# Moving the conditioning products of a two-layer decoder between the weight pieces, in column-grouped units

## The chip, the cores and the metric

One core of a Trainium2 chip runs the whole program. The metric is the device time of one execution in microseconds. Three runs of the kernel before gave a median of 3252.13 us (3251.81 to 3252.35).

## The reference, cut to what matters

Two decoder layers run over 544 tokens: one prompt of 512 and eight sequences of four sample tokens. Each layer is a half-step SwiGLU feed-forward block (FFN1), a middle block (input projection, an RG-LRU recurrence, sparse attention with a top-k index, output projection) and a second half-step block (FFN2). Before each block the residual is normalised, scaled and shifted, and after each block a normalised result is added with a gate. The nine scale, shift and gate vectors of a layer come from one product with the conditioning vectors `c` (9 rows: the prompt and eight sequences):

```python
mod = (c @ w_ada_l + b_ada_l).reshape(c.shape[0], N_MOD, -1)
sh1, sc1, gt1, sh2, sc2, gt2, sh3, sc3, gt3 = [mod[:, m][:, None, :] for m in range(N_MOD)]
f = swiglu(rms_norm(x, g[0]) * (1 + sc1) + sh1, w_gu[0], w_dn[0])
x = x + 0.5 * gt1 * rms_norm(f, g[1])
h = rms_norm(x, g[2]) * (1 + sc2) + sh2
...
x = x + gt2 * rms_norm(y, g[3])
f = swiglu(rms_norm(x, g[4]) * (1 + sc3) + sh3, w_gu[1], w_dn[1])
x = x + 0.5 * gt3 * rms_norm(f, g[5])
```

All of it is float32; `D_MODEL` is 1024, `D_FF` 2816, `w_ada` is 1024 x 9216 in each layer.

## The kernel before, in words

Everything is kept transposed: features on the 128 partitions, the 544 tokens in the free dimension, in two halves of 272. All five engines run streams written by hand, tied by semaphores; the two layers are unrolled.

**Weight pieces.** A weight matrix is used in pieces of 128 columns. A piece is loaded by the SP queue (`piece`, L470 to L477) into one of four raw slots `wslot`. ScalarE rounds it to a high part `w_hi` (L874, `split`), VectorE subtracts to get a low part (L1110, `split`), and TensorE multiplies high by high, high by low and low by high (L581, L582, L583, in `piece`), for each of the two token halves and each of eight row chunks: 48 products of 272 columns. There are two high and two low buffers. SP loads a raw slot again when VectorE has made the low part from it (`w_split`, L476). A feed-forward block has 44 gate-up pieces (GU) and 24 down pieces (DN), the down pieces with 8, 8 and 6 row chunks for each of eight output columns. The input projection (IN) has 17 pieces and the output projection (OUT) eight.

**Ada.** `w_ada` goes through the same four raw slots, 72 pieces a layer. `ada_chunk` (L586 to L594) multiplies one piece with `c`: the stationary operand is `cT` (128 x 9), the moving one 128 columns of `w_ada`, eight products over the rows, plain float32. For each of the nine vectors VectorE copies the two halves of the result (L1198, `ada_half`), TensorE transposes them (L601), and VectorE adds the bias (L1204, `ada_bias`). The order is written out by hand: vectors 0 and 1 at the start of a layer (`ADA0`), 2 to 4 between GU and DN of FFN1 (`ADA1`, L624 `between()`), and 5 to 8 in the sample top-k loop of the attention (`ADA2`, L794 to L801, one chunk in each of the 32 iterations).

**Around the blocks.** After the last down piece TensorE sums the squares of the eight result chunks with a matrix of ones (`sums_of_squares`, L547 to L555, products at L553, plain float32), ScalarE takes the root (L858), VectorE the reciprocal and the residual (`residual`, L1138 to L1157), then the squares of the new `x` are summed the same way, and `pre_norm` (L1113 to L1136) writes the next block's moving operands chunk by chunk.

**The top-k loop.** VectorE runs 32 iterations of MAX8 (L1495) and MATCH_REPLACE8 (L1508) over the sample scores, with the prompt attention's masked maximum (L1488), `tile_output` (L1471), `ada_half` and `ada_bias` between them. After it come L1510, the last `tile_output`, the mask transposes (L807) and L1517.

**Queues.** SP issues nearly all loads in program order: `cT`, `x`, the constants and the page table, then the pieces, 16 small gate loads (L513), half of the key pages, and the value pages of three sequences (L531) with `ADA2` pieces between them. The POOL queue loads the other key and value pages.

Of the kernel before, what the change touches and what calls it, by code (L numbers as in the profile page):

```python
# [18 lines left out]
F32 = mybir.dt.float32  # L19
# [52 lines left out]
RING = 4  # L72
RPF = DC // RING
U_GU = FC // 2
DN_K = (8, 8, 6)


class Phase:


    full = [0] * RING
    ada = [0] * RING
    split = [0] * RING
    used = [0, 0]
    order = 0

    def __init__(self, rounds, per_round, slots, is_ada=False, tail=0):
        self.rounds, self.per_round, self.slots, self.tail = rounds, per_round, slots, tail
        self.full0, self.ada0, self.split0 = list(Phase.full), list(Phase.ada), list(Phase.split)
        self.used0, self.order0 = list(Phase.used), Phase.order  # L90
        for n in range(rounds * per_round + tail):
            i = n % slots
            Phase.full[i] += 1
            (Phase.ada if is_ada else Phase.split)[i] += 1
            if not is_ada:
                Phase.used[n % 2] += 1
                Phase.order += 1

    def has(self, u, n):

        return u * self.per_round + n < self.rounds * self.per_round + self.tail

    def raw(self, u, n):

        return n % self.slots, u * (self.per_round // self.slots) + n // self.slots

    def part(self, u, n):

        return n % 2, u * (self.per_round // 2) + n // 2


ADA0 = Phase(2 * RPF, RING, RING, is_ada=True)
GU1 = Phase(U_GU, RING, RING)
ADA1 = Phase(3 * RPF, RING, RING, is_ada=True)
DN1 = Phase(DC // 2, 2 * len(DN_K), len(DN_K))
IN = Phase(PC // RING, RING, RING, tail=1)
ADA2 = Phase(4 * RPF, RING, RING, is_ada=True)
OUT = Phase(DC // RING, RING, RING)
GU2 = Phase(U_GU, RING, RING)
DN2 = Phase(DC // 2, 2 * len(DN_K), len(DN_K))  # L120
PAGE_UNROLL = 4
ARENA = FC * T + 2048
KREC = PAGE + PAGE // 2


DVE_STEPS = 361
# [14 lines left out]
def hold(eng, passed, sem, value):  # L141


    eng.wait_ge(sem, value)
    eng.sem_inc(passed, 1)


class Steps:

    def __init__(self, eng, sem, per, layer, passed):
        self.passed = passed
        self.eng, self.sem, self.per, self.layer, self.n, self.shift = eng, sem, per, layer, 0, 0
# [7 lines left out]
    def need(self, n):  # L162

        self.eng.wait_ge(self.sem, self.layer * self.per + (n + self.shift))

    def need_hold(self, n):

        hold(self.eng, self.passed, self.sem, self.layer * self.per + (n + self.shift))
# [3 lines left out]

    def link_hold(self, ins):

        self.need_hold(self.mark(ins))

    @contextmanager
    def loop(self, times, body_steps, start=0):

        first = self.n  # L180
        with self.eng.Fori(start, start + times) as i:
            self.shift = i * body_steps + (-start * body_steps)
            yield i
        assert self.n - first == body_steps, (self.n - first, body_steps)
        self.n = first + times * body_steps
        self.shift = 0


def decoder(nc, a):

    with ExitStack() as ctx:
# [10 lines left out]
        wslot = [sb(f"wslot{i}", [P, DC, P]) for i in range(RING)]  # L202
# [17 lines left out]
        act_hi = part("act_hi", at_arena, FC, T)  # L220
        at_whi = at_arena + FC * T
        w_hi = [part(f"w_hi{i}", at_whi + i * DC * P, DC, P) for i in range(2)]
        h_hi = part("h_hi", at_proj, DC, T)
        h_lo = part("h_lo", at_h, DC, T)
        at_wlo = at_proj + DC * T
        w_lo_ffn = [part(f"w_lo_ffn{i}", at_wlo + i * DC * P, DC, P) for i in range(2)]
        at_tsil = at_wlo + 2 * DC * P
        at_alo = at_down + 2 * PAGES * KREC - FC * T
        assert at_tsil + 2 * T <= at_alo and at_whi + 2 * DC * P <= at_proj
        act_lo = part("act_lo", at_alo, FC, T)  # L230

# [3 lines left out]
        w_lo_mid = [part(f"w_lo_mid{i}", at_whi - (2 - i) * DC * P, DC, P) for i in range(2)]  # L235
        cst = sb("cst", [P, C_ALL])
        vec = sb("vec", [P, V_ALL])
        state = sb("state", [P, ST_ALL])
        cT = sb("cT", [P, DC, NC_])
        mod = sb("mod", [P, MC, NC_])  # L240
        modT = sb("modT", [NC_, DC, P])
# [7 lines left out]

        sq = proj[:, 0:DC, :]  # L250
        tsil = part("tsil", at_tsil, 2, T, dt=F32)
# [23 lines left out]
        assert at_arena + at[0] <= at_whi - 2 * DC * P  # L275
# [48 lines left out]
        w_full = [sig(f"w_full{i}", Phase.full[i], 16) for i in range(RING)]  # L324
        ada_used = [sig(f"ada_used{i}", Phase.ada[i]) for i in range(RING)]
        w_hi_done = sig("w_hi_done", Phase.order)
        w_split = [sig(f"w_split{i}", Phase.split[i]) for i in range(RING)]
        w_used = [sig(f"w_used{i}", Phase.used[i]) for i in range(2)]
        vec_full = sig("vec_full", 2, 16)
        vec_free = sig("vec_free", 1, 1, 1)  # L330
        gate_full = sig("gate_full", 16, 16)
# [10 lines left out]
        modT_ready = sig("modT_ready", 2 * NMOD)  # L342
        mod_pe = sig("mod_pe", NMOD)
        ada_read = sig("ada_read", NMOD, 1, 1)
# [6 lines left out]
        act_raw = sig("act_raw", 2 * FC)  # L351
# [4 lines left out]
        act_ready = sig("act_ready", 2 * FC, 1, 2)  # L356
# [54 lines left out]
        cleared = sig("cleared", 0)  # L411
        passed = [ctx.enter_context(nc.semaphore(f"passed_{e}")) for e in ("sp", "pe", "pool", "dve")]
# [29 lines left out]
        def key_loads(eng, on_sp, l, pair):  # L442


            who, first, after, full = ((passed[0], 0, KEYS_SP, kp_full) if on_sp
                                       else (passed[2], KEYS_SP, PAGES, kp_full_pool))
            if isinstance(pair, int):

                hold(eng, who, dn_read.sem, dn_read.at(l, DC))
            for i in range(2):  # L450
                hold(eng, who, kp_used[i].sem, kp_used[i].at(l, pair))
                load_pages(eng, a["key_pages"], l, pair * (2 * PAGES) + i * PAGES, first, after, kpage[i], full[i])
# [3 lines left out]
        def _(sp):  # L456
            sp.dma_start(cT[:, :, :], a["cT"]).then_inc(s_in.sem, 16)
            sp.dma_start(x[:, :, :], a["xT"]).then_inc(s_in.sem, 16)
            sp.dma_start(cst[:, :], a["cst"]).then_inc(s_in.sem, 16)
            sp.dma_start(pages[:, :], a["page_table"]).then_inc(s_in.sem, 16)  # L460
            sp.wait_ge(s_in.sem, 64)
            sp.wait_ge(cleared.sem, 1)
            for l in range(DEPTH):

                def rows(ap):
                    return ap.rearrange("a (c p) n -> p (a c) n", p=P)

                ada, w_in, w_out = (layer_of(a[n], l) for n in ("w_ada", "w_in", "w_out"))

                def piece(ph, u, n, src):  # L470

# [7 lines left out]
                def pieces(ph, src, first=0, start=0, rounds=None):  # L479

                    for u in range(start, start + (rounds or ph.rounds)):
                        for n in range(RING):
                            piece(ph, u, n, rows(src[:, :, bass.ds(u * (RING * P) + (first + n) * P, P)]))
# [1180 lines left out]
```

## Time and profile before

| | |
|---|---|
| median of three runs | 3252.13 us |
| the profiled execution | 3247.81 us |
| its span, first to last instruction | 3246.1 us |
| TensorE busy | 88% of the span, 20506 products |
| VectorE / ScalarE / GpSimd busy | 45% / 23% / 5% |
| granted TensorE clock, mean | 0.89 of full speed |
| DMA | 292.75 MB, 90 GB/s, 524771 packets |

A busy share says how much of the span had an instruction of that engine in flight; the ends of products are modelled. The profiled execution is 4.3 us (0.13%) shorter than the median. The execution falls into these stages in layer 0 (layer 1 repeats them from about 1627 us): start to 73.6, GU of FFN1 to 344.6, `ADA1` to 393.8, DN to 528, residual and norm to 570, IN to 687, recurrence and index products to 873, top-k loop to 1055, the rest of the attention to 1118, OUT to 1170, residual and norm to 1211, GU and DN of FFN2 to 1619.

### The profile page before, as it was taken

To read this page: it belongs to the slowest core of one execution; us is meant where nothing else is said; L and a number is where in the kernel's file an instruction comes from. 1 tells how busy PE (TensorE), PEld (TensorE's weight loads), DVE (VectorE), ACT (ScalarE), POOL (GpSimd) and SP (SyncE) were. 2 spreads that over 40 slices of the span, in tenths; PEclk is the share of its full clock that TensorE was granted. 3 is DMA by queue.
4 is the path that set the end of the run, shared out by engine and by line. 5 is a ranking of instruction groups with operands and counts; after the bars stand their busy time and mean duration, and the time that the engine had idled before them with its cause. 6 is when DMAs were issued, how large, how long until landed. Compare 5 with 4: busy or idle time off the path is not lost.

```text
span 3246.1 us, 49665 instructions
## 1 busy us (share of the span) xinstructions
PE 2854.9 (88%) x20506; PEld 2638.2 (81%) x20506; DVE 1465.4 (45%) x2006; ACT 734.3 (23%) x1038; POOL 158.8 (5%) x298
## 2 busy tenths in 40 slices
PE   5999997988778669999979999969796868699997
PEld 4999896976655669999969998969675548699997
DVE  2333124365799443332153331244648992533312
ACT  1222023230012132222222220222200222322221
POOL 0000001001420000000000000010114100000000
PEclk8999998975579789999999999989656889899998
DMA  6232623212353012222243326323124421132231
GB/s 186 83 88 86 183 87 85 73 40 64 115 152 111 20 46 84 86 87 76 87 130 88 89 85 184 90 68 83 48 67 127 141 83 46 39 91 86 71 90 64
DMA packets 524771, 292.75 MB, mean 90 GB/s; under 512 B 20673, under 2 KB 518882, under 8 KB 524162
## 3 DMA queue, kind: packets, MB, share of 16 engines
q1 hardware_dynamic: 513154, 266.35, 28.1%
q0 software_dynamic: 11392, 23.23, 2.4%
q8 instruction: 161, 2.64, 0.3%
q14 instruction: 64, 0.52, 0.1%
HBM read 285.75 MB, written 3.77 MB: 89 GB/s over the span
## 4 chain that ended last, share of the span: by engine, by line
PE 81%; DVE 14%; issue 3%; DMA 1%; ACT 1%; SPq 0%; DVEq 0%; ACTq 0%
PE ps L583 20%; PE ps L581 20%; PE ps L582 19%; PE ps L592 5%; PE ps L703 4%; PE ps L553 3%; DVE sb_arena L1495 3%; PE ps L701 3%; DVE sb_y L1508 3%; PE ps L819 2%; PE ps L563 1%; DMA sb_wslot<-w_ada 1%; DVE sb_h L1122 1%; PE ps L723 1%; DVE sb_h L1149 1%
## 5 line engine op out<-in xcount | busy, mean ns | idle before, releaser
L582 PE MATMUL ps<-sb_h_lo,sb_w_hi 128*128 128x272 f32 x3360 | 972.8, 290 | 0.0
L581 PE MATMUL ps<-sb_h_hi,sb_w_hi 128*128 128x272 f32 x2816 | 817.7, 290 | 54.6 <-DVE sb_h_lo L1135 54.6
L583 PE MATMUL ps<-sb_h_hi,sb_w_lo_ffn 128*128 128x272 f32 x2816 | 820.1, 291 | 0.0
L1110 DVE TENSOR_TENSOR sb_w_lo_ffn<-sb_wslot,sb_w_hi 128x1024 fp32r<-128x1024 f32 (+1 forms) x272 | 324.0, 1194 | 792.3 <-ACT sb_w_hi L874 792.1
L874 ACT ACTIVATE sb_w_hi<-sb_wslot 128x1024 fp32r<-128x1024 f32 (+2 forms) x322 | 332.8, 1036 | 1518.4 <-PE ps L583 1380.0
L582 PEld LDWEIGHTS ps<-sb_h_lo,sb_w_hi 128*128 128x128 f32 x3360 | 640.5, 191 | 0.5
L581 PEld LDWEIGHTS ps<-sb_h_hi,sb_w_hi 128*128 128x128 f32 x2816 | 534.3, 190 | 59.6 <-issue 53.8
L583 PEld LDWEIGHTS ps<-sb_h_hi,sb_w_lo_ffn 128*128 128x128 f32 x2816 | 533.8, 190 | 0.0
L581 PE MATMUL ps<-sb_act_hi,sb_w_hi 128*128 128x272 f32 x1408 | 408.5, 290 | 11.1 <-DVE sb_w_lo_ffn L1110 11.1
L583 PE MATMUL ps<-sb_act_hi,sb_w_lo_ffn 128*128 128x272 f32 x1408 | 407.9, 290 | 0.0
L582 PE MATMUL ps<-sb_act_lo,sb_w_hi 128*128 128x272 f32 x1408 | 407.4, 289 | 0.0
L592 PE MATMUL ps<-sb_wslot,sb_cT 128*9 128x128 f32 x2304 | 301.0, 294 | 20.6 <-DMA sb_wslot<-w_ada 20.5
L592 PEld LDWEIGHTS ps<-sb_wslot,sb_cT 128*9 128x9 f32 x2304 | 217.8, 98 | 87.0 <-issue 19.5
L581 PEld LDWEIGHTS ps<-sb_act_hi,sb_w_hi 128*128 128x128 f32 x1408 | 268.4, 191 | 11.6 <-issue 11.6
L582 PEld LDWEIGHTS ps<-sb_act_lo,sb_w_hi 128*128 128x128 f32 x1408 | 268.5, 191 | 0.0
L583 PEld LDWEIGHTS ps<-sb_act_hi,sb_w_lo_ffn 128*128 128x128 f32 x1408 | 268.4, 191 | 0.0
L1173 DVE SCALAR_TENSOR_TENSOR sb_tsil<-sb_tsil,ps 128x544 f32<-128x544 f32 x88 | 63.4, 721 | 276.3 <-PE ps L583 276.3
L581 PE MATMUL ps<-sb_h_hi_mid,sb_w_hi 128*128 128x272 f32 x544 | 162.3, 298 | 27.0 <-DVE sb_h_lo L1135 27.0
L433 POOL DMA_DIRECT2D sb_down<-key_pages x128 | 68.8, 538 | 1970.8 <-issue 1970.8
L703 PE MATMUL ps<-sb_arena,sb_down 128*128 128x32 f32 x512 | 161.6, 409 | 0.0
L583 PE MATMUL ps<-sb_h_hi_mid,sb_w_lo_mid 128*128 128x272 f32 x544 | 158.4, 291 | 0.0
L1495 DVE MAX8 sb_arena<-sb_y 32x8 f32<-32x2080 f32 x64 | 147.9, 2311 | 0.0
(217 smaller groups left out, 3152.0 us busy)
## 6 DMA issues: line engine op xcount, KB each, us to landing
sb_wslot<-ffn_w_gu SPq DMA_DIRECT2D x176, 512.0 KB, 3.6
sb_wslot<-w_ada SPq DMA_DIRECT2D x144, 512.0 KB, 4.8
sb_wslot<-ffn_w_down SPq DMA_DIRECT2D x64, 512.0 KB, 3.9
sb_wslot<-w_in SPq DMA_DIRECT2D x32, 512.0 KB, 3.8
sb_wslot<-ffn_w_down SPq DMA_DIRECT2D x32, 384.0 KB, 3.3
sb_down<-key_pages POOLq DMA_DIRECT2D x128, 96.0 KB, 2.2
sb_down<-key_pages SPq DMA_DIRECT2D x128, 96.0 KB, 1.9
sb_wslot<-w_out SPq DMA_DIRECT2D x16, 512.0 KB, 4.1
```

The source lines that it names most:

```text
L433: eng.dma_start(dst.rearrange("p a n -> p (a n)"), src).then_inc(full.sem, 16)
L553: last = mm(ps[:, 6 + b, 0:TH], ones, sq[:, c, b * TH:(b + 1) * TH], start=(c == 0), stop=(c == DC - 1))
L581: mm(out, wh, xh, start=(kc == 0), stop=False)
L582: mm(out, wh, xl, start=False, stop=False)
L583: last = mm(out, wl, xh, start=False, stop=(kc == of - 1))
L592: last = mm(ps[0:NC_, bank, i * P:(i + 1) * P], cT[:, kc, :], wslot[i][:, kc, :], start=(kc == 0), stop=(kc == DC - 1))
L701: mm(ps[0:HD, 4 + i, j * 32:(j + 1) * 32], kpage[i][:, j, P:KREC], qiS[:, bass.ds(pair * 2 + i, 1), :, :].rearrange("p a e c -> p (a e c)" ...
L703: last = mm(ps[:, 6 + i, j * 32:(j + 1) * 32], kpage[i][:, j, 0:P], qS[:, bass.ds(pair * 2 + i, 1), :].rearrange("p a c -> p (a c)"), star ...
L874: act_fn(w_hi[s][:, 0:rows, 0:cols], wslot[i][:, 0:rows, 0:cols], ACT.Copy).then_inc(w_hi_done.sem, 1)
L1110: v.tensor_tensor(w_lo[s][:, 0:rows, 0:cols], wslot[i][:, 0:rows, 0:cols], w_hi[s][:, 0:rows, 0:cols].bitcast(F32), ALU.subtract).then_inc ...
L1495: found = st.mark(v.max(top_s, scS))
L1508: replaced = st.mark(v.match_replace(scS, top_s, scS, TAKEN))
```

## The change

- Ada becomes 18 units of 512 columns a layer. A unit is 32 products: for each of eight row chunks, four products whose outputs lie on partitions 0 to 31, 32 to 63, 64 to 95 and 96 to 127. `cT` is padded to 32 columns. One VectorE copy of 128 x 128, one 128 x 128 transpose and one bias addition finish a unit.
- Units 0 to 3 run at the start of layer 0, each with its own buffer. Units 4 to 15 of each layer run in GU of FFN1, one behind every third piece. Units 16 and 17, and in layer 0 also the first four of layer 1, run in GU of FFN2, one behind every sixth piece. They share one 2 MB buffer `ada_w`; SP loads it again when the products of the unit before are done. A unit is transposed one piece later.
- `ADA1` and `ADA2` are gone from the gap behind GU and from the top-k loop.
- The low part of a piece overwrites its raw slot. There are three high buffers, and SP loads piece q when product q - 4 is done (`w_used`). Splits run two pieces ahead across the ends of blocks.
- Gate-up products use three pairs of PSUM banks and wait for the reads of the piece three before. DN waits for the activations that its first pieces need, not for all.
- In DN and OUT the squares of a result column are summed behind a piece of the next column; the last column's behind the last piece.
- Weights and `w_ada` are laid out by the host so that a piece or unit is one contiguous row for each partition; `vec` and `state` of both layers and the gates come in one load each. `hold` (a wait followed by a semaphore increment) becomes a plain wait.

```diff
+            def unit(n, pair):
+                buf = ada_first[n] if n < 4 else ada_w
...
                 for kc in range(DC):
-                    last = mm(ps[0:NC_, bank, i * P:(i + 1) * P], cT[:, kc, :], wslot[i][:, kc, :],
-                              start=(kc == 0), stop=(kc == DC - 1))
-                last.then_inc(ada_used[i].sem, 1)
+                    for g in range(4):
+                        last = mm(ps[32 * g:32 * (g + 1), 2 * pair, 0:P], cT[:, kc, :], buf[:, kc, g * P:(g + 1) * P],
+                                  start=(kc == 0), stop=(kc == DC - 1))
+                last.then_inc(ada_mm.sem, 1)
+            def unit_transpose(n, pair):
+                pe.wait_ge(ada_tok.sem, n + 1)
+                if n:
+                    pe.wait_ge(ada_done.sem, n)
+                nc.tensor.transpose(ps[:, 2 * pair + 1, 0:P], modT[:, :], ident).then_inc(ada_pe.sem, 1)
...
+            def ffn(l, f):
...
+                for n in range(GU_N):
+                    if n >= 3:
+                        pe.wait_ge(gu_read.sem, reads + n - 2)
+                    piece(q + n, 1 + n % 3, h_hi, h_lo, norm=2 * f if n == 0 else None)
+                    if n - 1 in units:
+                        unit_transpose(units[n - 1], 0)
+                    if n in units:
+                        unit(units[n], 0)
...
+                for n in range(DN_N):
+                    m, j = divmod(n, len(DN_K))
+                    k0 = sum(DN_K[:j])
+                    if m == 0:
+                        pe.wait_ge(act_ready.sem, act_ready.at(l, f * FC + k0 + DN_K[j]))
...
+                    piece(q + n, dn_pair(m), act_hi, act_lo, k0, FC)
+                    if m and j == 1:
+                        squares_of(m - 1, dn_read, l, f * DC)
+                squares_of(DC - 1, dn_read, l, f * DC).then_inc(ss_ready.sem, 1)
...
+                for n in range(OUT_N):
+                    pe.wait_ge(wo_read.sem, wo_read.at(l, n + 1 - 2))
+                    piece(l * PIECES + OUT + n, n % 2, y_hi, y_lo)
+                    if n:
+                        squares_of(n - 1, wo_read, l, 0)
+                squares_of(OUT_N - 1, wo_read, l, 0).then_inc(ss_ready.sem, 1)
-                sums_of_squares(wo_read, l, 0)
...
+            def unit(n):
+                if n > 4:
+                    sp.wait_ge(ada_mm.sem, n)
+                dst = ada_first[n] if n < 4 else ada_w
+                sp.dma_start(dst.rearrange("p c n -> p (c n)"), a["w_ada"][n // UNITS, n % UNITS])\
+                    .then_inc((ada_full0[n] if n < 4 else ada_full).sem, 16)
+            sp.dma_start(cT[:, :, :], a["cT"]).then_inc(c_in.sem, 16)
+            unit(0)
...
+            sp.dma_start(cst[:, :], a["cst"]).then_inc(s_in.sem, 16)
+            unit(1)
+            sp.dma_start(x[:, :, :], a["xT"]).then_inc(x_in.sem, 16)
+            unit(2)
+            unit(3)
...
+                def piece(q, src):
+                    rows, cols = shape_of(q)
+                    if q >= SLOTS:
+                        sp.wait_ge(w_used.sem, q - SLOTS + 1)
...
+                        if n - 1 in units:
+                            unit_bias(units[n - 1], 0)
+                        if n in units:
+                            unit_token(units[n], 0)
...
-                    if hd == 4:
-                        ada_half(5 + i, 0, ADA2, i * RPF + 1, 0)
-                    if i and hd == 0:
-                        ada_half(5 + i - 1, 1, ADA2, i * RPF, 0)
-                    if i and hd == 2:
-                        ada_bias(5 + i - 1, 1)
```

## Rows read from the trace of the kernel before

**Rows 1.** The page's part 4: the chain that ended last, by engine.

```profile
PE 81%; DVE 14%; issue 3%; DMA 1%; ACT 1%; SPq 0%; DVEq 0%; ACTq 0%
```

**Rows 2.** Busy times by stretch: length, PE, PEld, DVE, ACT, POOL, clock, DMA, GB/s.

```profile
78.00:344.00 266.00, 266.00 (x2096) 265.79 (x2095) 94.98 (x108) 68.78 (x86) 0.00 (x0) 0.99 0.29 84
344.00:392.00 48.00, 45.42 (x414) 36.60 (x412) 5.99 (x10) 1.75 (x3) 0.00 (x0) 1.00 0.86 249
```

**Rows 3.** Timeline of GU: start us, us, instruction; the last products of neighbouring pieces.

```profile
199.83 0.28 PE L583 MATMUL ps<-sb_h_hi,sb_w_lo_ffn 128*128 128x272 f32 x1
...
205.87 0.28 PE L583 MATMUL ps<-sb_h_hi,sb_w_lo_ffn 128*128 128x272 f32 x1
```

**Rows 4.** Timeline, layer 0: first product of `ADA1` and first of DN.

```profile
344.62 14.14 PE L592 MATMUL ps<-sb_wslot,sb_cT 128*9 128x128 f32 x128
...
393.84 0.47 PE L581 MATMUL ps<-sb_act_hi,sb_w_hi 128*128 128x272 f32 x1 [1.67 <-DVE sb_w_lo_ffn L1110]
```

**Rows 5.** Chain in order of time (start us, us), layer 1: the same two places.

```profile
1949.86 3.61 PE ps L592 x32
...
1997.89 0.36 PE ps L581
```

**Rows 6.** Chain: last product of GU, first two of DN, FFN2 of layer 0.

```profile
1480.24 0.14 PE ps L583
...
1484.23 0.57 PE ps L581
1484.80 0.23 PE ps L582
```

**Rows 7.** Timeline: sums of squares behind DN and the next block's first product, twice.

```profile
1619.41 7.49 PE L553 MATMUL ps<-sb_proj,sb_cst 128*128 128x272 f32 x32
...
1680.64 0.57 PE L581 MATMUL ps<-sb_h_hi,sb_w_hi 128*128 128x272 f32 x1 [13.06 <-DVE sb_h_lo L1135]
...
528.13 7.50 PE L553 MATMUL ps<-sb_proj,sb_cst 128*128 128x272 f32 x32
...
528.85 0.62 ACT L916 ACTIVATE sb_proj<-ps 128x544 f32<-128x544 f32 x1
...
569.63 0.56 PE L581 MATMUL ps<-sb_h_hi_mid,sb_w_hi 128*128 128x272 f32 x1 [13.06 <-DVE sb_h_lo L1135]
```

**Rows 8.** Timeline of VectorE: the top-k loop's first two iterations, and its end.

```profile
876.62 0.29 DVE L1488 CUSTOM_DVE_ANT_0 sb_arena<-ps,sb_arena 128x128 f32<-128x128 f32 x1 [1.05 <-PE ps L746]
...
881.60 0.27 DVE L1488 CUSTOM_DVE_ANT_0 sb_arena<-ps,sb_arena 128x128 f32<-128x128 f32 x1
...
1048.51 1.23 DVE L1510 TENSOR_SCALAR sb_y<-sb_y 32x2080 f32<-32x2080 f32 x1
...
1054.84 0.69 DVE L1517 COPY sb_rinv<-ps 128x512 f32<-128x512 f32 x1 [0.81 <-PE ps L808]
```

**Rows 9.** Timeline of the start: first use of `x`, sums of squares, first product.

```profile
12.46 4.48 ACT L853 ACTIVATE sb_proj<-sb_x 128x544 f32<-128x544 f32 x8 [9.54 <-DMA sb_pages<-page_table]
...
52.92 7.57 PE L553 MATMUL ps<-sb_proj,sb_cst 128*128 128x272 f32 x32 [0.42 <-DVE sb_mod L1204]
...
73.55 0.57 PE L581 MATMUL ps<-sb_h_hi,sb_w_hi 128*128 128x272 f32 x1 [13.06 <-DVE sb_h_lo L1135]
```

**Rows 10.** DMA issues by line: count, KB each, us from issue to landing.

```profile
sb_x<-xT SPq DMA_DIRECT2D x1, 2176.0 KB
sb_cst<-cst SPq DMA_DIRECT2D x1, 1072.0 KB
sb_wslot<-ffn_w_gu SPq DMA_DIRECT2D x176, 512.0 KB, 3.6
sb_vec<-vec SPq DMA_DIRECT2D x2, 76.0 KB, 1.8
```

**Rows 11.** Ada products: their group by line, and one chunk of 16 in `ADA1`.

```profile
L592 PE MATMUL ps<-sb_wslot,sb_cT 128*9 128x128 f32 x2304 | 301.0, 294 | 20.6 <-DMA sb_wslot<-w_ada 20.5
...
372.65 1.92 PE L592 MATMUL ps<-sb_wslot,sb_cT 128*9 128x128 f32 x16 [0.16 <-DMA sb_wslot<-w_ada]
```

More of the change, by code:

```diff
@@ L68, with dn_pair, shape_of @@
 ST_H, ST_C, ST_ALL = 0, LC * NSEQ, LC * NSEQ * 4
-RING = 4
-RPF = DC // RING
-U_GU = FC // 2
+SLOTS, HIS = 4, 3
+GU_N, DN_N, OUT_N = 2 * FC, 3 * DC, DC
 DN_K = (8, 8, 6)
[L78 to L120, printed above, removed]
+GU1 = 0
+DN1 = GU1 + GU_N
+IN = DN1 + DN_N
+OUT = IN + PC + 1
+GU2 = OUT + OUT_N
+DN2 = GU2 + GU_N
+PIECES = DN2 + DN_N
+UNITS = 18
+UNIT = 512
+UNITS_IN = [[(l * UNITS + 4 + i, 3 * i + 2) for i in range(12)] for l in range(DEPTH)], \
+           [[(l * UNITS + 16 + i, 6 * i + 5) for i in range(6) if l * UNITS + 16 + i < DEPTH * UNITS] for l in range(DEPTH)]
+def dn_pair(m):
+    return 1 + (m - 1) % 2 if m else 3
+def shape_of(q):
+    n = q % PIECES
+    if DN1 <= n < IN or n >= DN2:
+        return DN_K[(n - (DN1 if n < IN else DN2)) % len(DN_K)], P
+    return DC, LAST if n == OUT - 1 else P
 PAGE_UNROLL = 4
-ARENA = FC * T + 2048
+ARENA = 13928 + 88
 KREC = PAGE + PAGE // 2
-DVE_STEPS = 361
 class Signal:
@@ L162, in need @@
     def need(self, n):
-        self.eng.wait_ge(self.sem, self.layer * self.per + (n + self.shift))
-    def need_hold(self, n):
-        hold(self.eng, self.passed, self.sem, self.layer * self.per + (n + self.shift))
+        self.eng.wait_ge(self.sem, n)
     def link(self, ins):
         self.need(self.mark(ins))
[L173 to L186, printed above, removed]
 def decoder(nc, a):
@@ L323, in decoder @@
         s_in = sig("s_in", 0)
[L324 to L331, printed above, removed]
+        c_in = sig("c_in", 0)
+        x_in = sig("x_in", 0)
+        w_full = [sig(f"w_full{i}", 0) for i in range(SLOTS)]
+        w_hi_done = sig("w_hi_done", PIECES)
+        w_split = sig("w_split", PIECES)
+        w_used = sig("w_used", PIECES)
+        ada_full0 = [sig(f"ada_full0{i}", 0) for i in range(4)]
+        ada_full = sig("ada_full", 0)
+        ada_mm = sig("ada_mm", UNITS)
+        ada_tok = sig("ada_tok", UNITS)
+        ada_pe = sig("ada_pe", UNITS)
+        ada_done = sig("ada_done", UNITS)
+        gu_read = sig("gu_read", 2 * GU_N)
+        gate_full = sig("gate_full", 1, 16)
         KEYS_SP = 8
@@ L463, in _ @@
+            sp.dma_start(x[:, :, :], a["xT"]).then_inc(x_in.sem, 16)
+            unit(2)
+            unit(3)
             for l in range(DEPTH):
[L465 to L470, printed above, removed]
-                    i, k = ph.raw(u, n)
-                    is_ada = ph in (ADA0, ADA1, ADA2)
-                    before = (ph.ada0[i], k + ph.split0[i]) if not is_ada else (k + ph.ada0[i], ph.split0[i])
-                    hold(sp, passed[0], ada_used[i].sem, ada_used[i].at(l, before[0]))
-                    sp.wait_ge(w_split[i].sem, w_split[i].at(l, before[1]))
-                    sp.dma_start(wslot[i][:, 0:src.shape[1], 0:src.shape[2]], src).then_inc(w_full[i].sem, 16)
```

577 lines of the change are left out of this document (254 added, 323 removed).

## The prediction, made before the changed kernel had run

> **What bounds the kernel.** I read the chain that ended last first: TensorE holds 81% of it, VectorE 14% [rows 1]. Then the busy times by stretch: in the gate-up stage TensorE is busy in all of 266 us at a granted clock of 0.99, the 2.4 GHz level, while VectorE and ScalarE are at about a third and a quarter [rows 2]. The timeline gives its pace: two neighbouring pieces end 6.04 us apart, 0.1258 us for each of 48 products [rows 3]. So the pieces have no slack. Whatever is put between them lengthens the stage by its TensorE time, and faster loads or splits bring nothing there. Time is to be had only where TensorE stands, or works on Ada alone: the `ADA1` gap, the layer boundary, the gap ahead of DN in FFN2, the start, and the top-k loop, where VectorE's own chain sets the pace. A change of under 0.2% (6.5 us) can't be told from none.
>
> Durations are of the profiled execution: 3247.81 us, its span 3246.1 and 1.7 around it, 4.3 us under the median. I apply the differences to the median, 3252.1.
>
> **What goes.** *`ADA1`:* in layer 0 its first product starts at 344.62 and the first of DN at 393.84 [rows 4], 49.2 us; in layer 1 1949.86 to 1997.89 [rows 5], 48.0 us. DN then starts at the lower clock level, with products of 0.23 us as in [rows 6] for about 15 products, 1.5 us more each time. With the units elsewhere DN follows GU without a gap: 100.2 us gained. Its first piece needs eight activations, long made; its third needs the last, due some 2 us behind GU, 12 us early.
>
> *Layer boundary:* from the sums of squares to the next block's first product it takes 61.2 us with `ADA0` of layer 1 between, and 41.5 us where no Ada lies between [rows 7]: 19.7 us gained.
>
> *Ahead of DN in FFN2:* DN waits for the last activation and two splits, 1480.38 to 1484.23, and then runs 23 products at 0.23 instead of 0.126 [rows 6]: 3.85 + 2.3, twice, 12.3 us. The splits now run two pieces ahead across the block's end, so nothing takes the place of this wait.
>
> *Top-k loop:* 876.62 to 1048.51 is 171.9 us [rows 8]. An iteration without Ada is 4.98 us on the narrowest tile [rows 8], and each wider tile adds about 0.13, so 32 come to 165.5, with three tile outputs of 0.65 to 167.5: 4.4 us gained, by layer 1's count 3.4. Behind the loop 6.3 us pass until the mask is copied [rows 8]; without the last Ada half and its transposes about 4.5. Together 11.6 us for both layers. The 64 chunks there are 113 us of products (1024 records of 0.11 [rows 4]); VectorE's chain hid nearly all of it, so moving `ADA2` out gives little.
>
> *Start:* today `x` and the constants are in at 12.46, the sums of squares end at 60.5 and the first product starts at 73.55 [rows 9]. Of 3284 KB issued from 0.9 on, less the 1.8 us that a small load takes, the rate is some 336 KB/us [rows 9, 10]. Ahead of the end of unit 3 lie 11848 KB in the changed order, so it lands near 38; its products at the lower clock level take 7 us, the copy and transpose 1, the squares 7.6, and 13.1 us lie between their end and the first product as now: 66.7, 7 us gained. At the 249 GB/s of the `ADA1` stretch [rows 2] it would be 4 us lost; with quick products and loads 12 gained.
>
> **What comes.** *Squares:* 28 of the 32 records of 7.5 us [rows 7], 6.6 us, now lie between pieces of DN or OUT, where TensorE has no slack. Behind the last piece ScalarE's copy and square end 1.34 us after the old start [rows 7], then four records of 0.94: a tail of 2.4 instead of 7.5, 5.1 us shorter. Today's sums already hide ScalarE's last two operations, so this part loses 1.45 us, six times: 8.7 us.
>
> *Units:* 32 of 36 lie between pieces and add their TensorE time; this term decides. There are 2304 Ada records for 1152 products [rows 11], so a product is two records; 128 records take 14.14 us [rows 4], 0.11 each. A unit has 64. Upper end: column groups run one after the other, 32 x 0.221 = 7.07 us. Lower end: four products side by side, 1.77. No row shows column groups at once. I take the middle, 3.55: both records of one product write the same columns and must follow each other, and the records stand in program order in every timeline, so the second record of one product can run beside the first of the next, and no more; that is one product every 0.11 us instead of 0.22. To it I add 0.1 for going over to float32, 0.25 for coming back and 0.11 for the transpose, a record of 128 columns: an estimate of 0.45 from the pace of [rows 4], 0.2 to 1. A unit costs 4.0 us, 32 of them 128.
>
> The Trainium skill ("TensorEngine Tiling (Array Packing)", Key Properties) says that a change of tiling mode drains the engine, which speaks against 36 short units. By it each unit pays two drains; no row here shows one, and 0.45 us may be short.
>
> *Waits:* SP's load of unit k waits for the products of unit k - 1; behind it stand the next pieces. It has three pieces and a unit, 22 us, and in that time 2048 + 3 x 512 KB must pass, 162 KB/us, against 249 GB/s in [rows 2]: no wait. A piece is loaded when product q - 4 is done, three pieces (18 us) ahead; landing takes 3.6 us [rows 10], ScalarE's and VectorE's splits some 1 us each. If that cover were gone, every late piece would idle TensorE. VectorE now waits for a unit's products with the splits behind it in its queue, 4 us, while TensorE has two pieces (12 us) split. SP loses 144 Ada loads of 512 KB and has 36 of 2048 KB, 30 fewer small gate loads and no waits for Ada ahead of the value pages; they come earlier, but their products wait for the softmax chain behind the loop. POOL's queue is untouched, and all of this is costed at nothing.
>
> **Sum.** 100.2 + 19.7 + 12.3 + 11.6 + 7 - 8.7 = 142 gained, 128 paid: 14 us less, 3238. Break-even is 4.44 us for a unit.
>
> **Rivals.** *Four at once:* if the groups keep their own order and don't block each other, a unit is 1.77 + 0.45; 32 cost 71, the start gains 10, and the time is 3252 - 74 = 3178. For it: four groups use separate columns and outputs. Against it: the order of two-record products. The Trainium skill ("TensorE: Matmul & The Clock Gate", Part 3) says that products on different column tiles start some 4 ns apart and finish in program order; by its first half this rival is right, by its second the pairing of my forecast. No row here shows either.
>
> *One after the other, slower than before:* if the groups do not overlap, a unit is 7.07 + 0.45, 32 cost 241, the start gains nothing: 135 - 241, 3358. It decides from 4.44 us a unit. For it: the records of [rows 4] are all serial. Against it: their products share one column range, so they had to be.
>
> *Late units:* the loads run below 162 KB/us, as a quiet 512 KB load with 142 KB/us does alone [rows 10]; at 150 each of 24 rounds in GU of FFN1 takes 1.8 us longer, 43 us: 3281.
>
> That the squares are not hidden at all is in the sum.
>
> **Chances.** Forecast 0.47, four at once 0.25, serial 0.18, late 0.10. The forecast's own range, with a unit between 3.7 and 4.6 and the start between -4 and +12, is 3222 to 3266. The range 3174 to 3290 takes in the four-fold case and the late one and leaves out the serial one. Faster: 0.25 and three quarters of 0.47, 0.60; same 0.11; slower: serial, most of the late case and a little of the forecast, 0.29.
>
> **What would show it.** Right: the pace of a piece still 6.04 us; the unit's 64 records spaced 0.055 on average, about 4 us from the last product of a piece to the first of the next; DN directly behind GU, at the full clock; 41 us at the layer boundary; the loop near 167.5; squares between DN's pieces and a tail near 2.4. Wrong: a unit of 2.3 or 7.5 us, or TensorE waiting on `ada_w` or on splits.

## The result, and the profile after

The changed kernel takes 3162.22 us (median of four runs, 3160.63 to 3167.2) against 3252.24 for the kernel before in the same measurement: 90.0 us less, a ratio of 0.9725 with a 95% interval of 0.9708 to 0.9742. The forecast was 3238 with a range of 3174 to 3290, so the gain was over six times the one forecast, and the time lies below the range. The case that came true is the first rival, four products at once, priced at 3178 with a chance of 0.25.

The profiled execution of after has a span of 3158.8 us, 87.3 less than the one before. Put together from the first and last weight products of each stage, both kernels, all in us:

| stretch | before | after | difference |
|---|---|---|---|
| start to the first gate-up product | 73.6 | 56.8 | -16.7 |
| four gate-up stages | 1079.0 | 1149.3 | +70.3 |
| last gate-up to first DN product, four times | 106.1 | 0.5 | -105.6 |
| DN four times, OUT twice | 637.5 | 667.7 | +30.3 |
| result to next block inside a layer, four times | 166.8 | 146.3 | -20.6 |
| layer boundary | 61.4 | 37.4 | -23.9 |
| end | 29.9 | 25.1 | -4.8 |
| IN and attention, twice | 1092.0 | 1075.6 | -16.3 |

The chain that ended last, by engine, answers to [rows 1]: TensorE holds less of it and VectorE more.

```profile
PE 78%; DVE 17%; issue 3%; ACT 1%; DMA 1%; SPq 0%; ACTq 0%; DVEq 0%
```

TensorE's timeline in the gate-up stage of layer 0 (start us, us, instruction): one unit between two pieces, and the transpose a piece later.

```profile
118.75 0.29 PE L530 MATMUL ps<-sb_h_hi,sb_w_lo 128*128 128x272 f32 x1
118.97 1.95 PE L543 MATMUL ps<-sb_ada_w,sb_cT 128*32 128x128 f32 x64
120.85 0.39 PE L528 MATMUL ps<-sb_h_hi,sb_w_hi 128*128 128x272 f32 x1
...
127.00 0.27 PE L552 MATMUL ps<-sb_cst,sb_modT 128*128 128x128 f32 x1
...
139.04 0.29 PE L530 MATMUL ps<-sb_h_hi,sb_w_lo 128*128 128x272 f32 x1
```

The 64 records of a unit, which alone take 0.11 us each [rows 4], pass in 1.95 us. Between the last product of a piece and the first of the next lie 2.10 us instead of 0.126. From 118.75 to 139.04, a unit and three pieces, it is 20.29 us; three pieces at the pace of [rows 3] are 18.12. So a unit costs 2.17 us in all, and 32 of them 69.4; the stages grew by 70.3. The pieces between keep their 6.04.

The gap is 2.10 us at each of the 32 units, within 0.01, so none of them waited for its load, and the rival of late units is out. Only the four units of the start waited for loads.

Where DN follows, and behind DN, in layer 0 (the same timeline); it answers to [rows 4] and [rows 7]:

```profile
351.88 0.29 PE L530 MATMUL ps<-sb_h_hi,sb_w_lo 128*128 128x272 f32 x1
352.01 0.29 PE L528 MATMUL ps<-sb_act_hi,sb_w_hi 128*128 128x272 f32 x1
...
380.57 0.29 PE L530 MATMUL ps<-sb_act_hi,sb_w_lo 128*128 128x272 f32 x1
380.69 1.08 PE L493 MATMUL ps<-sb_sq,sb_cst 128*128 128x272 f32 x4
...
381.74 0.28 PE L529 MATMUL ps<-sb_act_lo,sb_w_hi 128*128 128x272 f32 x1
...
491.08 0.29 PE L530 MATMUL ps<-sb_act_hi,sb_w_lo 128*128 128x272 f32 x1
492.59 1.19 PE L493 MATMUL ps<-sb_sq,sb_cst 128*128 128x272 f32 x4 [1.23 <-ACT sb_sq L833]
505.27 9.70 PE L493 MATMUL ps<-sb_sq,sb_cst 128*128 128x272 f32 x32 [11.49 <-ACT sb_sq L787]
528.10 0.56 PE L528 MATMUL ps<-sb_h_hi_mid,sb_w_hi 128*128 128x272 f32 x1 [13.12 <-DVE sb_h_lo L1035]
```

DN starts 0.13 us behind gate-up, and its first product takes 0.29 us, not the 0.47 of [rows 4]: the gap and the cold start are both gone. A column's squares push the next products back: 380.57 to 381.74 is 1.17 us where two products take 0.25, so 0.92 a column. Behind the last piece only the last column's four records are left. The two idle times there, 11.49 us ahead of the squares of `x` and 13.12 ahead of the next block, are TensorE waiting for ScalarE and VectorE.

### The profile page after: what moved, and what is told of

It reads as the page before. It is cut to its first block, busy times and chain, and to the rows that moved or that the text cites. A ratio compares the mean times of both kernels' runs of the same rounds, so it can differ in the third digit from the quotient of the medians.

```text
span 3158.8 us, 48554 instructions
## 1 busy us (share of the span) xinstructions
PE 2704.0 (86%) x20398; PEld 2524.9 (80%) x20398; DVE 1440.7 (46%) x2023; ACT 734.9 (23%) x1038; POOL 159.0 (5%) x298
## 4 chain that ended last, share of the span: by engine, by line
PE 78%; DVE 17%; issue 3%; ACT 1%; DMA 1%; SPq 0%; ACTq 0%; DVEq 0%
PE ps L528 20%; PE ps L530 20%; PE ps L529 20%; PE ps L650 5%; DVE sb_arena L1382 4%; DVE sb_y L1389 4%; PE ps L493 3%; PE ps L648 3%; PE ps L543 2%; PE ps L754 2%; PE ps L510 1%; DVE sb_h L1022 1%; PE ps L670 1%; DVE sb_h L1046 1%; DMA sb_ada_first<-w_ada 1%
## 5 line engine op out<-in xcount | busy, mean ns | idle before, releaser
L530 PE MATMUL ps<-sb_h_hi,sb_w_lo 128*128 128x272 f32 x2816 | 819.3, 291 | 0.0
L1012 DVE TENSOR_TENSOR sb_w_lo<-sb_wslot,sb_w_hi 128x1024 fp32r<-128x1024 f32 (+2 forms) x322 | 383.0, 1191 | 582.9 <-ACT sb_w_hi L809 582.9
L530 PEld LDWEIGHTS ps<-sb_h_hi,sb_w_lo 128*128 128x128 f32 x2816 | 534.6, 190 | 0.0
L530 PE MATMUL ps<-sb_act_hi,sb_w_lo 128*128 128x272 f32 x1408 | 407.6, 290 | 0.0
L530 PEld LDWEIGHTS ps<-sb_act_hi,sb_w_lo 128*128 128x128 f32 x1408 | 264.7, 188 | 0.0
L1084 DVE SCALAR_TENSOR_TENSOR sb_tsil<-sb_tsil,ps 128x544 f32<-128x544 f32 x88 | 63.4, 721 | 431.0 <-PE ps L530 431.0
L1080 DVE SCALAR_TENSOR_TENSOR sb_tsil<-sb_tsil,ps 128x544 f32<-128x544 f32 x88 | 63.5, 721 | 308.4 <-ACT sb_tsil L822 308.4
L703 PEld LDWEIGHTS ps<-sb_cst,sb_arena 128*128 128x128 f32 x160 | 27.0, 209 | 191.8 <-ACT sb_arena L917 191.8
L825 ACT ACTIVATE sb_act_hi<-sb_tsil 128x544 fp32r<-128x544 f32 x88 | 58.2, 662 | 492.3 <-DVE sb_tsil L1084 492.3
L703 PE MATMUL ps<-sb_cst,sb_arena 128*128 128x128 f32 x160 | 50.9, 442 | 132.4 <-ACT sb_arena L917 132.4
```

Of the source, the lines that this page charges most:

```text
L530: last = mm(out, wl[:, r, :], xh, start=False, stop=(kc == of - 1))
L703: last = nc.tensor.transpose(ps[:, 6 + n % 2, j * P:(j + 1) * P], prob[n % 2][:, j * P:(j + 1) * P], ident)
L1012: v.tensor_tensor(w_lo[q % SLOTS][:, 0:rows, 0:cols], wslot[q % SLOTS][:, 0:rows, 0:cols], w_hi[q % HIS][:, 0:rows, 0:cols].bitcast(F32), ...
```

## The experiments

Two questions were open: why a unit costs half of what was forecast, and whether the other terms of the sum held, which their stages in the table mix.

### The units: which products run side by side

Five kernels change only the order, the output groups or the number of a unit's products (and, with the output groups, the copies that read them). The lines are one unit of the kernel's gate-up stage (TensorE's timeline), between the last product of a piece and the first of the next.

**One group after the other.**

```diff
-                for kc in range(DC):
-                    for g in range(4):
+                for g in range(4):
+                    for kc in range(DC):
```

> The eight products of one column group follow each other, then those of the next group; data, count and outputs are as in the changed kernel (3162 us; a unit costs 2.17 us there over three pieces, 1.97 of it from the last product of the piece to the first of the next). Theory S, products run side by side where their neighbours in program order go to other column groups: a unit falls back to 64 records of 0.11 us, 7.1 us, so 32 units cost about 165 us more and the start some 10 more, 3335 us. Theory Q, each column group keeps a queue of its own and the order between groups does not matter: 3162 us, a unit still near 2.0. Theory W, the records are shorter for another reason (32 stationary columns, the contiguous buffer) and nothing overlaps: 3162 us as well.

Measured: 3297.22 us, ratio to before 1.0148 (1.0107 to 1.0189).

```profile
110.76 0.29 PE L530 MATMUL ps<-sb_h_hi,sb_w_lo 128*128 128x272 f32 x1
110.97 5.96 PE L543 MATMUL ps<-sb_ada_w,sb_cT 128*32 128x128 f32 x64
116.86 0.39 PE L528 MATMUL ps<-sb_h_hi,sb_w_hi 128*128 128x272 f32 x1
```

The gap is 6.10 us. The order alone makes the change slower than the kernel before, so theories Q and W fall; but S missed by 38 us, since something still overlaps. The same list, cut off 0.03 us behind a unit's first record, shows four records started in the changed kernel and one here:

```profile
118.97 0.32 PE L543 MATMUL ps<-sb_ada_w,sb_cT 128*32 128x128 f32 x4
```

```profile
110.97 0.30 PE L543 MATMUL ps<-sb_ada_w,sb_cT 128*32 128x128 f32 x1
```

**One group only.**

```diff
-                for kc in range(DC):
-                    for g in range(4):
-                        last = mm(ps[32 * g:32 * (g + 1), 2 * pair, 0:P], cT[:, kc, :], ...
+                for g in range(4):
+                    for kc in range(DC):
+                        last = mm(ps[0:32, 2 * pair, g * P:(g + 1) * P], cT[:, kc, :], ...
```

The order is that of the run before; VectorE copies the four ranges one by one.

> All 32 products of a unit go to partitions 0 to 31, in four ranges of 128 columns, and VectorE makes four copies of 32 rows instead of one of 128. Theories S and Q (column groups side by side): no two products can overlap, a unit takes 7.1 us, the time is about 3335 us. Theory W (a record is simply shorter with this operand and buffer): a unit stays near 2.0 us and the time near 3162.

Measured: 3337.32 us, ratio 1.0271 (1.0229 to 1.0313).

```profile
112.09 0.29 PE L530 MATMUL ps<-sb_h_hi,sb_w_lo 128*128 128x272 f32 x1
112.31 7.17 PE L543 MATMUL ps<-sb_ada_w,sb_cT 128*32 128x128 f32 x64
119.41 0.39 PE L528 MATMUL ps<-sb_h_hi,sb_w_hi 128*128 128x272 f32 x1
```

A gap of 7.32 us: with the same operands and buffer the records take their 0.11 us each again. The column groups are the cause, not the shape. Nor is it the change of output: this kernel moves to another range of columns at the three places where the run before moves to another group, and in its trace all 64 records of the unit start one by one, 0.11 us apart (the second 0.13).

**Two groups at a time.**

```diff
-                for kc in range(DC):
-                    for g in range(4):
-                        last = mm(...)
+                for g0 in range(2):
+                    for kc in range(DC):
+                        for g in (g0, g0 + 2):
+                            last = mm(...)
```

> Products alternate between groups 0 and 2 for all eight row chunks, then between 1 and 3. Theory S: two at a time, a unit takes 3.55 + 0.2 = 3.75 us, 32 of them cost 57 us more than now and the start about 4: 3223 us; this is also the price that the prediction gave to four groups in program order. Theory Q: still four at a time, 3162 us. Theory W: 3162 us.

Measured: 3208.17 us, ratio 0.9874 (0.9836 to 0.9911).

```profile
124.58 0.29 PE L530 MATMUL ps<-sb_h_hi,sb_w_lo 128*128 128x272 f32 x1
...
128.01 0.39 PE L528 MATMUL ps<-sb_h_hi,sb_w_hi 128*128 128x272 f32 x1
```

Two-fold, with a gap of 3.43 us instead of the 3.75 of theory S, whose time lies 15 us too high.

**Every product twice.**

```diff
-                for kc in range(DC):
+                for kc in range(2 * DC):
...
+                        (operands and start, stop by kc % DC)
```

> Every unit makes its 32 products twice, in the same order of groups, the second time over the first result. If a unit is 1.77 us of products (64 records of 0.11 us, four at a time) and 0.40 us of fixed cost (going over, coming back, the transpose), 32 units cost 57 us more and the last unit of the start 2: 3221 us. If the whole 2.17 us grows with the products: 69 us more, 3233.

Measured: 3221.81 us, ratio 0.9923 (0.9899 to 0.9947).

```profile
149.45 0.29 PE L530 MATMUL ps<-sb_h_hi,sb_w_lo 128*128 128x272 f32 x1
149.66 3.70 PE L543 MATMUL ps<-sb_ada_w,sb_cT 128*32 128x128 f32 x128
153.29 0.39 PE L528 MATMUL ps<-sb_h_hi,sb_w_hi 128*128 128x272 f32 x1
```

The gap grows from 2.10 to 3.84, so 32 products are 1.74 us, and 2.10 - 1.74 - 0.126 = 0.23 is the price of going over and coming back. With that price off, the one-group unit is 7.32 - 0.126 - 0.23 = 6.96 us, four times 1.74: the overlap is four-fold in full. The rest of the 2.17 us, 0.20, stands at the transpose and the piece behind it.

The first three runs now fit one number. Each of the three changes of group in the first run saved (7.32 - 6.10) / 3 = 0.41 us. With two groups at a time there is one change: 6.96 / 2 - 0.41 + 0.36 = 3.43, the gap measured. The single records of the first run, which the view merges, show where it comes from. The first twelve records of group 0 start alone, 0.11 us apart; beside each of its last four starts one of the first four of the next group, at most 0.03 us behind it, and so at each of the three changes: four times 0.109, less 0.03, is 0.41. So it looks as if the next group may start once no more than three records wait behind the one that runs. The next run tests that.

**Runs of two products of a group.**

```diff
-                for kc in range(DC):
-                    for g in range(4):
-                        last = mm(...)
+                for k2 in range(0, DC, 2):
+                    for g in range(4):
+                        for kc in range(k2, k2 + 2):
+                            last = mm(...)
```

> Two products of a column group in turn, then two of the next, so four groups are visited in runs of two products (0.44 us). Strict neighbours, a product runs only beside the one right before it on another group: about 3.75 us from piece to piece in place of 2.1, 32 of them 53 us, 3217. Look-ahead, from the 0.41 us that each of three changes of group saved where the groups followed in turn (7.32 to 6.10 us) and from 3.43 us with two groups: a record that waits for its own group lets about 0.4 us of later records pass it by, so runs of two products still overlap nearly four-fold: 2.1 to 2.6 us, 3163 to 3180.

Measured: 3163.61 us, ratio 0.9732 (0.9708 to 0.9756).

```profile
118.87 0.29 PE L530 MATMUL ps<-sb_h_hi,sb_w_lo 128*128 128x272 f32 x1
...
121.04 0.39 PE L528 MATMUL ps<-sb_h_hi,sb_w_hi 128*128 128x272 f32 x1
```

A gap of 2.17 us. Strict neighbours are out by 53 us, the look-ahead holds.

**No units in the gate-up stages.**

```diff
-                units = {n: k for k, n in UNITS_IN[f][l]}
+                units = {}
```

The units' loads, copies, transposes and biases are left out with them, and the vectors that they would make are zero.

> Left out: the 32 units between the pieces, with their loads, copies and transposes; only vectors 0 and 1 of layer 0 are computed, the others are zero. If the units cost what the cadence of the pieces shows (8.02, 6.17 and 6.10 us against three of 6.04: 2.17 us each) and hide nothing, 69 us less than the changed kernel: 3094. If they also slow the pieces about them through their loads or VectorE's queue: less than 3085. If part of them lies where TensorE would wait anyway: over 3105.

Measured: 3093.53 us, ratio 0.9514 (0.9495 to 0.9532), 70.8 us below the 3164.36 that the changed kernel took in the set of runs below. The cadence's 69.4 is the price within 1.4 us, less than the changed kernel's runs differ among themselves; no cost of the loads or of VectorE's queue shows beside it.

### The other terms: squares, plain waits, start

**The changed kernel again**, as the measure for the three that follow.

> The changed kernel as it is, beside the next three on one chip: 3162 us (3160 to 3167).

Measured: 3164.36 us (3161.83 to 3164.64, five runs), ratio 0.9729 (0.9710 to 0.9749).

**Squares behind the last piece again.**

```diff
-                    if m and j == 1:
-                        squares_of(m - 1, dn_read, l, f * DC)
-                squares_of(DC - 1, dn_read, l, f * DC).then_inc(ss_ready.sem, 1)
+                sums_of_squares(dn_read, l, f * DC)
```

and the same for OUT.

> The squares of DN and OUT are summed behind the last piece again, all eight columns, as in the kernel before; the rest is as changed. Theory of the prediction: between the pieces they cost TensorE 6.6 us in each of six places and shorten the tail by 5.1, so taking this part back gains 8.7 us: 3153. Theory from the trace of the changed kernel: a column's four records lengthen DN by 0.71 us (0.84 from the last product before to the first behind, less 0.126), seven of them 5.0, and the tail is 4.6 to 5.4 shorter, so the part is worth nothing either way: 3162, within 3.

Measured: 3156.83 us (3156.3 to 3158.68), ratio 0.9710 (0.9691 to 0.9730): 7.5 us less than the changed kernel, whose five runs all lie above. The prediction's theory holds, and the one read from the trace after falls. Behind DN in layer 0 of this kernel:

```profile
488.48 0.29 PE L530 MATMUL ps<-sb_act_hi,sb_w_lo 128*128 128x272 f32 x1
488.60 7.50 PE L493 MATMUL ps<-sb_sq,sb_cst 128*128 128x272 f32 x32
...
530.59 0.57 PE L528 MATMUL ps<-sb_h_hi_mid,sb_w_hi 128*128 128x272 f32 x1 [13.13 <-DVE sb_h_lo L1031]
```

The tail is 42.1 us against 37.0 (491.08 to 528.10), 5.1 longer. But DN takes 132.74 us here against 139.07, 6.3 shorter, OUT 5.4. The misreading: 0.71 a column ends at the start of the next product (0.84 behind 380.57), but the one behind that still starts late, at 381.74; a column costs the 0.92 read above, seven of them 6.4. Nor did the length of DN show it: DN before was itself 1.4 us (layer 0's FFN2 2.3) longer than 132.74, since it began with slow products; after minus before so showed only 4.0 to 5.0 in three of the four.

**Waits with an increment again**, in VectorE's top-k parts.

```diff
-                    st.need(found)
+                    st.need_hold(found)
```

`need_hold` is `need` followed by `sem_inc(dve_passed, 1)`. The increment stands also at the two other waits of an iteration, and at two in the prompt's rounds.

> In the two top-k parts VectorE's plain waits become waits followed by an increment of a semaphore again: three in each of 32 iterations, and two kinds in the prompt's rounds. Theory: an increment costs VectorE some 0.04 us; the iteration goes back from 4.86 to 4.98 us, 32 of them twice are 7.7 us, with the prompt's rounds up to 9: 3170 to 3171. Rival, the iteration is shorter because the Ada work has left the loop: 3162.

Measured: 3171.12 us (3167.78 to 3173.53), ratio 0.9755 (0.9735 to 0.9774): 6.8 more than the changed kernel. VectorE's timeline, first the changed kernel's loop and what follows it, then this one's first iteration and the end of its loop:

```profile
830.88 0.29 DVE L1375 CUSTOM_DVE_ANT_0 sb_arena<-ps,sb_arena 128x128 f32<-128x128 f32 x1 [0.89 <-PE ps L693]
...
833.34 0.12 DVE L1384 TENSOR_SCALAR sb_arena<-sb_arena 128x1 f32<-128x1 f32 x1
833.45 0.08 DVE L1389 MATCH_VALUE_LOAD sb_y<-sb_arena,sb_y 32x8 f32 x1
...
835.75 0.27 DVE L1375 CUSTOM_DVE_ANT_0 sb_arena<-ps,sb_arena 128x128 f32<-128x128 f32 x1
...
995.03 1.23 DVE L1391 TENSOR_SCALAR sb_y<-sb_y 32x2080 f32<-32x2080 f32 x1
...
1002.04 0.69 DVE L1394 COPY sb_rinv<-ps 128x512 f32<-128x512 f32 x1 [3.10 <-PE ps L743]
```

```profile
834.89 0.29 DVE L1382 CUSTOM_DVE_ANT_0 sb_arena<-ps,sb_arena 128x128 f32<-128x128 f32 x1 [1.05 <-PE ps L698]
...
837.35 0.12 DVE L1391 TENSOR_SCALAR sb_arena<-sb_arena 128x1 f32<-128x1 f32 x1
837.57 0.08 DVE L1396 MATCH_VALUE_LOAD sb_y<-sb_arena,sb_y 32x8 f32 x1
...
839.87 0.27 DVE L1382 CUSTOM_DVE_ANT_0 sb_arena<-ps,sb_arena 128x128 f32<-128x128 f32 x1
...
1002.39 1.23 DVE L1398 TENSOR_SCALAR sb_y<-sb_y 32x2080 f32<-32x2080 f32 x1
```

The iteration is 4.98 us again, as in [rows 8], against 4.87, and the 0.11 lies at one place: MATCH_VALUE_LOAD starts 0.22 us behind TENSOR_SCALAR where it was 0.11; its loop takes 167.5 us (834.89 to 1002.39), which is the forecast's number to the tenth, against 164.15. So the loop's 7.7 us in layer 0 have two causes: 4.4 from the Ada work that left, 3.35 from the plain waits.

**Squares of `x` ahead of unit 2 at the start.**

```diff
                     for n in range(4):
+                        if n == 2:
+                            sums_of_squares(sq_ready, l, 0)
                         unit(n, n % 3)
...
-                sums_of_squares(sq_ready, l, 0)
+                else:
+                    sums_of_squares(sq_ready, l, 0)
```

with the root ahead of ScalarE's splits, VectorE's reciprocal ahead of the bias of unit 2, and the second low part behind the norm.

> In the start of layer 0 TensorE sums the squares of x ahead of unit 2 instead of behind unit 3, ScalarE takes the root ahead of its two splits, VectorE makes the reciprocal between units 2 and 3, and the second low part goes behind the norm. Theory: the start is bound by the chain unit 3 landed at 33.3, squares 7.5, root, reciprocal 3.6, norm; squares and reciprocal then lie beside the loads, and the first gate-up product starts 6 to 8 us earlier than at 56.84: 3155. Rival, VectorE's own chain (token, bias, reciprocal, splits) takes its place: under 2 us gained.

Measured: 3157.42 us (3156.79 to 3157.77), ratio 0.9711 (0.9692 to 0.9730), 6.9 less than the changed kernel. The start of the changed kernel, then of this one:

```profile
33.35 1.96 PE L543 MATMUL ps<-sb_ada_first,sb_cT 128*32 128x128 f32 x64 [1.11 <-DMA sb_ada_first<-w_ada]
...
56.84 0.57 PE L528 MATMUL ps<-sb_h_hi,sb_w_hi 128*128 128x272 f32 x1 [13.13 <-DVE sb_h_lo L1035]
```

```profile
24.23 9.29 PE L493 MATMUL ps<-sb_sq,sb_cst 128*128 128x272 f32 x32 [2.51 <-ACT sb_sq L790]
...
50.72 0.57 PE L528 MATMUL ps<-sb_h_hi,sb_w_hi 128*128 128x272 f32 x1 [10.35 <-DVE sb_h_lo L1039]
```

The squares run from 24.23, ahead of units 2 and 3, and the first product starts 6.1 us earlier.

### A version that beats both

A unit costs 2.17 us between pieces, and TensorE stands 11 and 13 us in every gap between blocks. Ten units fit there.

```diff
+            def sums_between_units(n, pair, l, k):
+                unit(n, pair)
+                sums_of_squares(sq_ready, l, k)
+                unit_transpose(n, pair)
+                unit(n + 1, pair)
...
                 ffn(l, 0)
-                sums_of_squares(sq_ready, l, 8)
+                sums_between_units(GAP_IN[l], 2, l, 8)
```

The same stands behind OUT and at the layer boundary. VectorE copies the first unit behind the residual; behind the norm it adds that unit's bias and copies the second. SP issues their loads, the second's behind the first pieces of the next block.

> Ten of the 32 units leave the gate-up stages for the gaps between blocks: one behind the last squares of a block's result, one between the squares of x and the next block's first product, in the five places where a block follows. TensorE stands idle there for some 10 and 13 us, and the load of the second (8.3 us) fits between. Theory: a unit between pieces costs its 2.17 us and one in a gap nothing: 22 us less than the changed kernel, 3141. Rival: the gaps are chains of VectorE and ScalarE that the copies and bias additions lengthen, or the second unit's load is late: half or less, 3152 or more.

Measured: 3143.38 us (3139.45 to 3145.71), ratio 0.9666 (0.9648 to 0.9683): 21.0 less than the changed kernel.

```profile
490.41 0.29 PE L542 MATMUL ps<-sb_act_hi,sb_w_lo 128*128 128x272 f32 x1
...
493.04 1.95 PE L555 MATMUL ps<-sb_ada_w,sb_cT 128*32 128x128 f32 x64
504.60 9.63 PE L505 MATMUL ps<-sb_sq,sb_cst 128*128 128x272 f32 x32 [9.61 <-ACT sb_sq L812]
...
514.27 1.95 PE L555 MATMUL ps<-sb_ada_w,sb_cT 128*32 128x128 f32 x64
527.36 0.56 PE L540 MATMUL ps<-sb_h_hi_mid,sb_w_hi 128*128 128x272 f32 x1 [11.13 <-DVE sb_h_lo L1060]
```

The gap is 36.95 us with two units in it, against 37.02 without; TensorE's idle times shrank from 11.49 and 13.12 to 9.61 and 11.13.

The last kernel takes this, the start, and the squares behind the last piece together; its diff is those three.

> The units in the gaps, the squares of x ahead of unit 2 at the start (6.9 us less when done alone), and the squares of DN and OUT behind the last piece (7.5 us less when done alone). Theory: the three lie in different places and add up, 3164 - 22 - 7 - 7.5: 3127. Rival: with the squares behind the last piece the first unit of a gap waits behind them and takes TensorE's time ahead of the squares of x, so that the gaps gain less: 3135 or more.

Measured: 3127.76 us (3124.12 to 3129.63), ratio 0.9619 (0.9603 to 0.9635): 36.6 us less than the changed kernel, where the single gains of 21.0, 6.9 and 7.5 sum to 35.4. They add up.

## Why the prediction was wrong

By its own steps, in us, gains positive; what is shown is read from the stages of both kernels and, for the squares, from the run that took them back:

| term | forecast | shown |
|---|---|---|
| `ADA1` and DN's cold start | 100.2 | 100.3 (97.5 and 2 x 1.4) |
| layer boundary, without the squares' part | 19.7 | 19.9 |
| ahead of DN in FFN2 | 12.3 | 10.6 (8.1 and 2.3 + 0.2) |
| top-k loop and what follows it | 11.6 | 13.3 |
| start | 7 | 16.7 |
| squares | -8.7 | -7.5 |
| 32 units | -128 | -69.4 |
| the remaining stretches | 0 | about 3 |

In layer 1 the DN of FFN2 before began with 16 slow products, which cost 1.6 us, but its other products went at 0.1245 us instead of 0.1257 and gave most of it back; so the 2.3 that the prediction read in layer 0 and counted twice came once. Why they were quicker no run shows.

**The step that failed** is the price of a unit: "both records of one product write the same columns and must follow each other, and the records stand in program order in every timeline, so the second record of one product can run beside the first of the next, and no more". It gave 3.55 us of products, and they take 1.74. The fixed part was sized well (0.45 against 0.43). A list sorted by start says nothing of whether two records overlap, and the rows ahead of the prediction had no two products on different column groups. The lower end, 1.77, was the truth; the choice of the middle cost 59 of the 76 us by which the forecast missed. The other 17 were smaller terms, the start above all: with a unit at 2.17 us the prediction's own sum gives 3179, still above the time, and the rival's 3178 missed by 16 for much the same terms. The run with two groups shows what the middle would have looked like (3.43 in a gap), and the run with the groups in turn that order does decide, though only beyond some 0.41 us.

The rule of the Trainium skill that spoke for this rival ("TensorE: Matmul & The Clock Gate", Part 3: products on different column tiles start some 4 ns apart) agrees with the 1.74 us: in the trace the records start in fours, 6 to 7 ns apart within a four and 0.11 us from four to four. Its other half, a strict order of starts and ends, would with two records a product leave the pairing of the forecast; the gaps of 2.10 and 2.17 us do not show such a pairing, and with the groups in turn the next group's first record starts ahead of three that stand before it in the program. The drain at a change of mode ("TensorEngine Tiling (Array Packing)", Key Properties) is bounded here: going over and coming back cost 0.23 us together.

**The start** was mis-sized by 9.7 in two terms. Unit 3 was in at 33.35, not at 38. Windows of the start (length, PE, PEld, DVE, ACT, POOL, clock, DMA, GB/s), after, then before:

```profile
10.00:15.00 5.00, 3.49 (x64) 3.04 (x60) 0.29 (x1) 0.00 (x0) 0.00 (x0) 1.00 1.04 444
```

```profile
5.00:10.00 5.00, 0.00 (x0) 0.00 (x0) 0.00 (x0) 0.00 (x0) 0.00 (x0) 1.00 0.98 419
10.00:15.00 5.00, 0.00 (x0) 0.00 (x0) 0.00 (x0) 2.54 (x5) 0.00 (x0) 1.00 0.33 114
```

The 336 KB/us of the forecast spread 3284 KB over all the time up to 12.46, but the engines had moved 419 GB/s from 5 to 10 us and then paused, 114 from 10 to 15. With the four units queued among the constants and `x`, 444 go on there. And the last unit took 1.96 us, not 7. (The prediction's bound of 4 us lost at 249 GB/s comes to over 5 by its own terms.)

**The top-k loop** was right for the wrong reason: Ada's leaving gave 4.4 and 3.1 us where 4.4 and 3.4 were forecast (164.15 + 3.35 = 167.5 in layer 0). The plain waits, costed at nothing by not being named, gave 6.8 in both layers together. Against that, what follows the loop takes 7.0 us (995.03 to 1002.04) instead of the 4.5 forecast, in both layers. That the two errors, some 7 us gained and 5 lost, nearly cancel is luck.

**Right:** the pieces' pace, `ADA1`, the boundary, the FFN2 gap within 2 us, no late unit or split, and the squares as a loss. That this part of the change costs 7.5 us is shown by taking it back. What stays open are the 3 us of the remaining stretches, which no run separated.

## What to carry to other kernels

When one unmeasured duration decides the sign, and its bounds are a factor of four apart, say which end each mechanism gives, and do not take a middle that needs a mechanism of its own. Here 32 small float32 products on four column groups overlapped in full when neighbours in program order changed group at every product, and all but 0.07 us of it when they changed at every second; eight in a row lost 4.0 of the 5.2 us that the overlap is worth, which made the change a loss. Before paying for work on the engine that bounds a stage, look for the gaps in which that engine waits for others: of the 21.7 us that ten units cost between pieces, 21.0 came back there.

## What was not expected of the hardware

A change of column group saved 0.41 us where eight products of a group stand in a row, and runs of two products cost only 0.07 us a unit more than single ones: in these runs TensorE's order between column groups is loose over four records, the one that runs and three that wait. What in the engine sets the four, no run shows.

With the Ada products gone from the loop, TensorE's granted clock is lower there. The windows of the loop and of the 7 us behind it (columns as above), after, then before:

```profile
831.00:995.00 164.00, 97.94 (x300) 64.30 (x300) 163.89 (x198) 36.58 (x99) 26.36 (x50) 0.50 0.15 47
995.00:1002.00 7.00, 5.97 (x35) 5.30 (x34) 2.13 (x3) 0.89 (x2) 0.00 (x0) 0.50 0.00 0
```

```profile
877.00:1048.00 171.00, 138.85 (x822) 93.92 (x823) 167.88 (x206) 36.53 (x99) 25.66 (x48) 0.83 0.46 133
1048.00:1055.00 7.00, 5.61 (x57) 4.60 (x56) 3.57 (x7) 0.95 (x3) 0.00 (x0) 1.00 0.27 78
```

TensorE is busy in 97.94 of 164 us instead of 138.85 of 171, and the granted clock in the loop fell from 0.83 to 0.50, the 1.2 GHz level, and behind it from 1.00 to 0.50. VectorE's chain hides that inside the loop; behind it the last tile's products and the mask transposes stand on the path, and VectorE's copy at 1002.04 waited 3.10 us for them where it had waited 0.81 [rows 8]. The same 4 and 16 records take 1.12 and 1.91 us there where they took 0.66 and 1.15. That the clock is what makes those 7.0 us is argued from these rows; no run tried it.

Of three waits with an increment in an iteration, only the one between two short instructions cost anything, 0.11 us; the other two stand beside MAX8 and MATCH_REPLACE8 of 2.3 us and were not seen.
